# The expert stage's shift summed by VectorE instead of TensorE, in the projections of a diffusion trunk

## What is computed

```python
sh1, sc1, g1, sh2, sc2, g2 = adaln(cond, w_mod, b_mod)   # silu(cond) @ w_mod + b_mod, split in six
mix = mixer(modulate(rms_norm(x, g_attn), sh1, sc1))     # projections, heads A, B, C, output projection
x = x + g1 * mix
x = x + g2 * hier_moe(modulate(rms_norm(x, g_ffn), sh2, sc2))
```

## Time and profile before

| | us |
|---|---|
| median of 3 runs | 1699.66 |
| lowest, highest of the 3 | 1699.25, 7877.1 |
| the profiled execution | 1700.76 |
| its span, first to last instruction | 1698.9 |
| TensorE busy | 1592.4 (94%) |
| VectorE busy | 690.6 (41%) |
| ScalarE busy | 262.5 (15%) |
| GpSimd busy | 105.6 (6%) |

### The profile page before, as it was taken

One profiled execution on the slowest core, in us unless ns is written; L12 is line 12 of the kernel. 1 busy time (PEld: TensorE's weight loads), 2 busy tenths in 40 slices (PEclk: granted clock), 3 DMA queues, 4 the chain that ended last, 5 costly groups with the idle time before them and its releaser, 6 DMA issues.

```text
span 1698.9 us, 18207 instructions
## 1 busy us (share of the span) xinstructions
PE 1592.4 (94%) x6671; PEld 653.5 (38%) x6716; DVE 690.6 (41%) x1361; ACT 262.5 (15%) x705; POOL 105.6 (6%) x191
## 2 busy tenths in 40 slices
PE   4999999999999999999999998999999989999998
PEld 2445555544434444443332332333333233233332
DVE  2112232213245794443453344345344443534444
ACT  2003222112123010011101101111110110111010
POOL 1022100010020100000000000000000000000000
PEclk9999999999999999999999999999999999999999
DMA  9995642734199766589999999999999999999996
GB/s 367 385 341 220 230 192 65 265 111 181 68 359 406 266 264 254 187 340 426 427 429 427 429 426 427 427 426 428 428 424 428 427 425 424 428 426 426 419 427 246
DMA packets 92638, 581.94 MB, mean 343 GB/s; under 512 B 9113, under 2 KB 24313, under 8 KB 55385
## 3 DMA queue, kind: packets, MB, share of 16 engines
q1 hardware_dynamic: 84944, 554.20, 80.2%
q0 software_dynamic: 5920, 22.63, 3.6%
q10 hardware_dynamic: 1728, 4.51, 0.7%
HBM read 584.06 MB, written 7.05 MB: 348 GB/s over the span
## 4 chain that ended last, share of the span: by engine, by line
PE 67%; DMA 17%; DVE 4%; issue 1%; ACT 1%; SPq 0%; POOL 0%; ACTq 0%
PE bank L1284 23%; DMA ring<-in_w 17%; PE bank L1032 13%; PE bank L1011 7%; PE bank L1194 7%; PE bank L1317 3%; DVE r L1778 2%; PE bank L906 2%; PE bank L1119 2%; PE bank L1243 2%; PE bank L1180 1%; PE bank L1266 1%; PE bank L992 1%; PE bank L1094 1%; PE bank L1102 1%
## 5 line engine op out<-in xcount | busy, mean ns | idle before, releaser
L1284 PE MATMUL bank<-ring,r 128*64 128x512 f32 x1920 | 469.2, 618 | 45.1 <-DMA ring<-in_w 45.1
L1284 PEld LDWEIGHTS bank<-ring,r 128*64 128x64 f32 x1920 | 129.6, 139 | 302.8 <-issue 302.8
L1032 PE MATMUL bank<-ring,r 128*128 128x384 f32 (+1 forms) x672 | 240.7, 516 | 0.0
L1998 DVE TENSOR_TENSOR bank<-bank,r 128x512 f32<-128x512 f32 x180 | 125.9, 700 | 265.7 <-PE bank L1194 265.7
L1317 PE MATMUL bank<-ring,mod_row 128*64 128x512 f32 x896 | 195.8, 593 | 8.1 <-ACT mod_row L1531 7.9
L1011 PE MATMUL bank<-ring,r 128*128 128x512 f32 x384 | 170.0, 595 | 0.0
L1032 PEld LDWEIGHTS bank<-ring,r 128*128 128x128 f32 x672 | 126.1, 190 | 102.9 <-issue 43.2
L1194 PE MATMUL bank<-r 128*128 128x512 bf16 x495 | 137.6, 382 | 7.2 <-issue 7.2
L2000 DVE TENSOR_TENSOR r<-r,bank 128x512 f32<-128x512 f32 x180 | 123.6, 687 | 6.2
L1317 PEld LDWEIGHTS bank<-ring,mod_row 128*64 128x64 f32 x896 | 75.2, 137 | 119.0 <-issue 108.9
L1194 PEld LDWEIGHTS bank<-r 128*128 128x128 bf16 x540 | 38.0, 97 | 167.4 <-DVE r L2000 96.5
(11 more groups left out here) (279 smaller groups left out, 1249.9 us busy)
## 6 DMA issues: line engine op xcount, KB each, us to landing
ring<-in_w SPq DMA_DIRECT2D x180, 2048.0 KB, 18.1
ring<-in_w_mod SPq DMA_DIRECT2D x96, 1024.0 KB, 14.1
ring<-in_w SPq DMA_DIRECT2D x19, 1024.0 KB, 10.1
ring<-in_w_o SPq DMA_DIRECT2D x16, 1024.0 KB, 7.3
ring<-in_w_in SPq DMA_DIRECT2D x20, 768.0 KB, 13.3
ring<-in_w_in SPq DMA_DIRECT2D x8, 1024.0 KB, 6.0
r<-mod_d POOLq DMA_DIRECT2D x8, 1024.0 KB, 9.1
r<-in_w SPq DMA_DIRECT2D x5, 1024.0 KB, 8.3
```

The costliest lines, as they stand in the source:

```text
L1032: mm = pe.matmul(acc[acc_of(a)][:, 0:w], h_t[:, k, t * P:(t + 1) * P], wu[:, j, :], start=(k == 0), stop=(k == KD - 1))
L1284: mm = pe.matmul(ps[64 * c:64 * c + 64, :], xg_t[:, j, 64 * c:64 * c + 64], big_cut(slot_of(u), (8, 512))[:, j % 8, :], start=(j == 0), st ...
L1998: v.tensor_tensor(ps[:, :], ps[:, :], g2b[:, min(t, 1), cols], ALU.mult).then_inc(strip_scaled, 1)
```

## The change

SH2 leaves TensorE's modulation steps, and `LATER_GROUPS` becomes (G1, SH2, SC2). Sixteen steps ("sh2", k) stand in the list instead, each directly behind a projection job (its norm where that comes at once, and the turn due then): one behind every tile of cq1, aq0, bq0, akv and bq1, and one behind aq1 tile 2. VectorE does two multiply-adds 128x2048 in each, as for G2. The two partial sums live in two ring slots, which GpSimd sets to zero and starts with the bias rows, and which are kept out of the ring from cq1's first weights until ten units behind the fold; the ring has ten slots meanwhile (`ring_plan` instead of `ring_slot`). With two groups left in `later`, the three steps in cq1 tiles 1 and 2 and the two behind aq0 tile 1 are gone, and `mods(2)` before a group of heads is `mods(1)`. After the last A heads, a step "fold" has TensorE sum both over the partitions with eight products into `mod_ps`; VectorE copies the result and GpSimd stores it.

```diff
-LATER_GROUPS = (SH2, G1, SC2)
+LATER_GROUPS = (G1, SH2, SC2)
+SH2_AT = {"cq1": (1, 1, 1), "aq0": (1, 1, 1), "aq1": (0, 0, 1), "bq0": (1, 1, 1), "akv": (1, 1, 1), "bq1": (1, 1, 1),
+          "bkv": (0, 0, 0)}
...
-def ring_slot(m):
+def ring_plan(n, held_from, held_to):
+
+    def run(names):
+        at, prior, order, last, held = [], [], list(names), {}, []
+        for m in range(n):
+            if m == held_from:
+                held, order = order[:2], order[2:]
+            if m == held_to:
+                order = held + order
+            s = order.pop(0)
+            order.append(s)
+            at.append(s)
+            prior.append(last.get(s))
+            last[s] = m
+        return at, prior, order, held
...
-    later = [(g, k) for g in LATER_GROUPS for k in range(KD)]
+    later = [(g, k) for g in LATER_GROUPS if g != SH2 for k in range(KD)]
+    sh2 = iter(range(KD))
...
             n = len(jobs) - 1
+            for k in [next(sh2) for _ in range(SH2_AT[name][t])]:
+                units.append(("mod", SH2, k))
+                steps.append(("sh2", k))
             if name == "cq1":
...
-                else:
-                    mods(3)
                 job("proj", ("cq0", t))
                 kvc(t + 1, 0)
                 kvc(t + 1, 1)
             else:
-                mods(2 if attends and (name, t) != ("bkv", 2) else 0)
+                mods(1 if attends and (name, t) not in (("bkv", 2), ("aq0", 1)) else 0)
...
     assert not scored and not turned_p
+    steps.append(("fold", SH2))
+    held_to = len(units) + SLOTS - 2
     steps.append(("cache", "b"))
...
+    held_from = unit_no[("first", FIRST_GROUPS[1], 3, 3)] + 1
...
+        sh2_sum = [ring[:, s, :] for s in held]
...
+        def emptied(m):
+
+            if m >= held_to and prior[m] < held_from and slots[m] in held:
+                return row_out, 2 * 32
+            return frees[prior[m]]
...
-                if m >= SLOTS:
-                    sp.wait_ge(*frees[m - SLOTS])
+                if prior[m] is not None:
+                    sp.wait_ge(*emptied(m))
...
+            def fold_sh2():
+
+                pe.wait_ge(*frees[unit_no[("mod", SH2, KD - 1)]])
+                pe.wait_ge(mod_read, 1)
+                for c in range(2):
+                    for q in range(4):
+                        mm = pe.matmul(mod_ps[32 * q:32 * q + 2, :], K("sel")[:, c:c + 2], sh2_sum[c][:, q * 512:(q + 1) * 512],
+                                       start=(c == 0), stop=(c == 1))
+                mm.then_inc(mod_done, 1)
...
+            def sh2_step(k):
+
+                m = unit_no[("mod", SH2, k)]
+                if k == 0:
+                    v.wait_ge(sh2_rows_in, 2 * 16)
+                v.wait_ge(*full_of(m))
+                for c in range(2):
+                    if c and k:
+                        v.wait_ge(*frees[unit_no[("mod", SH2, k - 1)]])
+                    last = v.scalar_tensor_tensor(out=sh2_sum[c], in0=ring[:, slots[m], :], scalar=csil[:, k, c:c + 1],
+                                                  in1=sh2_sum[c], op0=ALU.mult, op1=ALU.add)
+                    if c == 0:
+                        after(last)
+                last.then_inc(*done_of(m))
...
+                elif s[0] == "fold":
+                    v.wait_ge(mod_done, 2)
+                    v.tensor_copy(sh2_sum[0][:, 0:512], mod_ps[:, :]).then_inc(mod_read, 1)
...
             load_row(LATER_GROUPS[0])
+            for slot in held:
+                g.wait_ge(*frees[max(m for m in range(held_from) if slots[m] == slot)])
+            g.memset(sh2_sum[0], 0.0)
+            after(g.memset(sh2_sum[1], 0.0))
+            for c in range(2):
+                g.dma_start(sh2_sum[c][0:1, :], b_rows[SH2:SH2 + 1]).then_inc(sh2_rows_in, 16)
...
+                elif s[0] == "fold":
+                    g.wait_ge(mod_read, 2)
+                    for c in range(2):
+                        g.dma_start(mod_d[SH2, c].rearrange("(q n) -> q n", q=4), sh2_sum[0][c:P:32, 0:512]).then_inc(row_out, 16)
```

More of the change, by code:

```diff
@@ L79 @@
 FOLD_AT = 6
-RING_FROM = 8
-def ring_slot(m):
-    return (m + RING_FROM) % SLOTS
+def ring_plan(n, held_from, held_to):
[12 more added lines that the diff above has]
+        return at, prior, order, held
+    end = run(range(SLOTS))[2]
+    name = [end.index(s) for s in range(SLOTS)]
+    at, prior, end, held = run(name)
+    assert end == list(range(SLOTS))
+    return at, prior, held
 def const_layout():
@@ L296, in plan @@
     assert g2_k == KD
-    return steps, jobs, atts, units
+    return steps, jobs, atts, units, held_to
 IN_NAMES = ["x_prompt", "x_sample", "cache_a_k", "cache_a_v", "cache_b_k", "cache_b_v", "cache_c_kv",
@@ L310, in build @@
 def build(nc, ins, outs):
-    steps, jobs, atts, units = plan()
+    steps, jobs, atts, units, held_to = plan()
     lay, n_const = const_layout()
@@ L315, in build @@
     n_static = len(units)
+    held_from = unit_no[("first", FIRST_GROUPS[1], 3, 3)] + 1
+    slots, prior, held = ring_plan(n_static + FIRST_UNITS - (EXTRA[1] - EXTRA[0]), held_from, held_to)
     n_jobs, n_atts = len(jobs), len(atts)
@@ L668, in build @@
                     else:
-                        slot_uses[ring_slot(u)] += 1
+                        slot_uses[slots[u]] += 1
         uses = [0] * SLOTS
@@ L672, in build @@
             if u not in frees:
-                uses[ring_slot(u)] += 1
-                frees[u] = (slot_free[ring_slot(u)], uses[ring_slot(u)])
+                uses[slots[u]] += 1
+                frees[u] = (slot_free[slots[u]], uses[slots[u]])
         assert uses == slot_uses
@@ L684, in build @@
                 done = [unit_no[("mod", G2, s[1])]]
+            elif s[0] == "sh2":
+                done = [unit_no[("mod", SH2, s[1])]]
             elif s[0] in ("proj", "kvc", "out"):
@@ L716, in build @@
             else:
-                slot_uses[ring_slot(m)] += 1
-                frees[m] = (slot_free[ring_slot(m)], slot_uses[ring_slot(m)])
+                slot_uses[slots[m]] += 1
+                frees[m] = (slot_free[slots[m]], slot_uses[slots[m]])
         def first_place(u):
             if u in first_no:
-                return ring[:, ring_slot(first_no[u]), :]
+                return ring[:, slots[first_no[u]], :]
             return extra[u - EXTRA[0]]
@@ L731, in small_free @@
         def small_free(u):
-            slots = (2 * slot_of(u), 2 * slot_of(u) + 1)
-            return [frees[max(m for m in frees if ring_slot(m) == slot)] for slot in slots]
+            pair = (2 * slot_of(u), 2 * slot_of(u) + 1)
+            return [frees[max(m for m in frees if slots[m] == slot)] for slot in pair]
         def moe_free(u, m):
@@ L1007, in out_part @@
                 arrived(m)
-                wu = cut(ring_slot(m), (4, 512))
+                wu = cut(slots[m], (4, 512))
                 for j in range(4):
@@ L1015, in out_part @@
                 elif t == TILES - 1:
-                    mm.then_inc(slot_free[ring_slot(m)], 1)
+                    mm.then_inc(slot_free[slots[m]], 1)
             a = 0
@@ L1777, in g2_step @@
                         v.wait_ge(*frees[unit_no[("mod", G2, k - 1)]])
-                    last = v.scalar_tensor_tensor(out=g2_sum[:, c, :], in0=ring[:, ring_slot(m), :], scalar=csil[:, k, c:c + 1],
+                    last = v.scalar_tensor_tensor(out=g2_sum[:, c, :], in0=ring[:, slots[m], :], scalar=csil[:, k, c:c + 1],
                                                   in1=g2_sum[:, c, :], op0=ALU.mult, op1=ALU.add)
+                    if c == 0:
[11 more added lines that the diff above has]
+                                                  in1=sh2_sum[c], op0=ALU.mult, op1=ALU.add)
                     if c == 0:
```

44 lines of the change are left out of this document (24 added, 20 removed).

## The result

The changed kernel takes 1717.47 us in the median of 4 runs (1716.74 to 1721.43), the kernel before 1700.57 beside it (one of its four executions took 7877.1 us; the median of the other three is 1699.66): ratio 1.0104, 95% interval 1.0088 to 1.012. That is 17 us or 1% slower, in the range of the prediction and 4.8 us above its point. The profiled execution took 1717.73 us around a span of 1715.9, 17.0 more than before.

A forecast was written before the change was run, and what follows sets the result against it. TensorE bounds the kernel up to the experts, the weight stream in them. Delays 3.6 + 0.9 + 4.1 + 4.1, less 0.5, 0.1 and 6.0, plus fold 1.8 and clock 5.1, give 13.0 us slower: 1712.7 us, range 1704 to 1719.

The forecast's parts named there:

- The three delays: In cq1's tiles 0, 1, 2, VectorE's blocks make norms late for TensorE's transposes: 3.6 plus 0.9, 4.1 and 4.1 us.
- GpSimd held, 0.9: In cq1 tile 0, kvc (0,0)'s rstd on GpSimd is held to the block's end, delaying the norm another 0.9 us.
- The clock, 5.1: Behind cq1's three new long TensorE waits the clock falls, 1.7 us each, 5.1 us in all.
- What is won back, 6.6: Steps removed from TensorE gain 0.5 us at first C heads, 0.1 before first A heads, 6.0 in seven other pairs.
- the other seven halves of pairs give 0.86 each: Where one of two consecutive SH2 steps leaves TensorE, seven places each save 0.86 us, 6.0 us together.
- some 5: Sign of being right: from the first C heads to the last A heads some 5 us are won back.
- The fold, 1.8: After the last A heads, TensorE's eight products summing the partial sums add 1.8 us, with no wait counted.
- The slots, 0: Ten ring slots from cq1's weights to the fold cost 0; bq0 tightest, but the DMA row is low there.
- GpSimd held in cq1's tiles 1 and 2 too: Rival: GpSimd is held there by one multiply-add each, 4.7 us more, 1717.4 us; chance 0.07.
- weights late: Rival: ten slots leave bq0 waiting 2.7 us, and blocks past the fold as much again, 1718 us; chance 0.08.
- the clock didn't hold: Refers to the rival that the clock holds around cq1's waits, leaving 7.9 us, 1707.6 us; chance 0.25.
- The relief that wins: Rival: no block reaches TensorE at cq1's transposes, so 14.1 less 1.8 us stays saved, 1687.4 us; chance 0.1.

The follow-up runs named there:

- the short fillers: Changed kernel plus idle TensorE products, fewer than the waits are long (3 or 6), ahead of five turns in cq1's stage: 1714.2 us, ratio 1.0081.
- the blocks ahead: Changed kernel with cq1's three blocks summed by VectorE ahead of the next projection's products instead of between a projection's results and their transposes: 1702.64 us, ratio 1.0003.
- the first block ahead: Changed kernel with only cq1's first block moved ahead of cq1 tile 1's products, those of tiles 1 and 2 staying: 1715.09 us, ratio 1.0088.
- the same with own turns: Changed kernel with cq1's three blocks moved ahead, and heads waiting only for ScalarE's copy of their own kind's last turn: 1700.86 us, ratio 0.9995.
- the waits filled too long: Changed kernel with 6, 10 and 10 idle TensorE products in its three long cq1 waits: 1725.78 us, ratio 1.014.

## Why the prediction held, point by point

**The three delays** (3.6 + 0.9, 4.1, 4.1). Bare, they are 3.94, 4.04 and 4.03 us. Tiles 1 and 2 are right to 0.1, though the removed steps, which I had at 0.7 us net of waiting, gave 0.49 and 0.51 when they alone were taken away. Moving the blocks shows the cause. Of the forecast's own signs, the projection that started at 173.40 starts 9.6 us later (8 or more), and the waits were 5.29, 4.41 and 3.63 us in the first profile (4 to 5), but 5.28, 2.70 and 2.72 in the second, where the slow clock filled part of them.

**GpSimd held, 0.9.** The mechanism is there (0.27 to 2.25 us, and 2.72 for the next), the price too high. I had the first operation held to the block's end and its 1.0 us of successors behind it. In the trace one operation is long beside each multiply-add, so they ran beside the block and the norm started at 153.81, 0.2 us behind the key's part that I had at 153.6. Beside the 3.6, 0.3 is left for this term in the bare 3.94. The rule of the Trainium skill, SBUF — State Buffer, "Who interferes with whom", that a VectorE instruction with two SBUF inputs and a GpSimd one that reads SBUF exclude each other for an instruction's length, agrees with the trace: both operations' lengths, 2.25 and 2.72 us, are near one multiply-add's 2.35.

**The clock, 5.1.** This term was mis-sized: 6.9 in one profile, 6.1 in the next. Three falls of 1.7 had been assumed; against the short fillers a stretch lost 0.0 to 3.0, and behind the third long wait the fall reaches into the next projection. I had priced the long waits alone; the clock also fell behind the wait of 2.15 us that was left in tiles 1 and 2, once in the first profile and twice in the second.

**What is won back, 6.6.** The step that failed is "the other seven halves of pairs give 0.86 each". In the changed kernel one gives 0.85 (bq1's tile 1), six 0.28 to 0.38, together 2.75 instead of 6.0. Their second step had covered ScalarE's copy of the turn, for which the first score waits by the plan. With that wait loosened all six are worth 0.85 or 0.86. The first C heads gave 0.23 instead of 0.5, bq1's tile 0 gave 0.34 instead of 0.1. All in all 3.3 (I had 6.6, and "some 5" among the signs).

**The fold, 1.8.** 1.68: from the fold's start to the output projection it took 41.12 us; the same piece before, from the cache turn at 492.85 us, which stands there without a fold, took 39.44. The fold's row took what G2's took the earlier trace rows:

```profile
508.41 1.90 PE L1014 MATMUL bank<-ring,cst 128*2 128x512 f32 x16
```

**The slots, 0.** Right for the changed kernel, where TensorE waits for no transfer there. But in the kernel before ten slots made it wait 0.78 us in bq0, so the argument "the DMA row is low there" was not a safe one.

**The sum.** A to D: 5.34 + 4.41 + 7.06 + 2.12 = 18.9; less 3.3; plus 1.7: 17.3. The first product of the output projection starts at 549.53 instead of 532.29, 17.24 later, and from there to the end the two profiles take 1166.4 and 1166.6 us: the shift is carried to the end one to one, as assumed. That they agree to 0.2 us is luck, since this last part took from 1164.4 to 1170.7 us in the twelve profiles, and 1169.1 in the changed kernel's second. Against the forecast's 13.0 that is 4.3 too much: 3.3 of relief that did not come and 1.8 of clock, less 0.7 in the three delays (12.0 instead of 12.7) and 0.1 in the fold.

The two large errors point the same way, so they didn't cancel: 1717.5 lies near the upper edge of the range and outside the forecast's own 1709 to 1716.

**The rivals.** By the time alone the rivals at 1717.4 (GpSimd held in cq1's tiles 1 and 2 too) and 1718 (weights late) fit better than the forecast; the traces rule them out. In tile 1 a GpSimd operation is indeed held, but VectorE goes on with cq0's norm as soon as the block is over, and the two stretches without the clock's part are 4.04 and 4.03 us longer, where I had 4.1 without it. These are GpSimd's row and VectorE's, block and norm:

```profile
175.76 2.60 POOL L2180 TENSOR_TENSOR small<-small,cst 128x2 f32<-128x2 f32 x1
...
175.46 4.74 DVE L1837 SCALAR_TENSOR_TENSOR ring<-ring,csil 128x2048 f32<-128x2048 f32 x2
180.12 1.01 DVE L1870 SCALAR_TENSOR_TENSOR r<-r,small,gains 128x64 f32<-128x64 f32 x4
```

TensorE waited for no weights, and the clock didn't hold. The relief that wins, priced at 14.1 - 1.8 = 12.3 us, is much smaller even where no block is in the way: with the blocks ahead the five stretches are 3.3 us shorter than before, and the output projection starts 2.5 sooner. In the whole time not even that shows (1.0003, 0.9993 to 1.0013); where it goes behind the projections stays open.

## What to carry to other kernels

Work moved to an engine that is busy 45% of the time is priced by its place in that engine's order: the same block cost 4 us between a norm and its transposes, and nothing ahead of the products. Work removed from the busiest engine is worth only what no other engine needs: ask for each removed piece which copy or norm it covered (here 0.5 of 2.7 us and 0.3 to 0.4 of 0.86 were left), and loosen or move that wait with it. Where the gain is under 0.3%, compare stretches of the profile; the whole time hides it, and a gain in a stretch may not reach the end.

## What the runs showed of the hardware

A wait costs twice. Behind the waits of 5.29, 4.41 and 3.63 us in the changed kernel's first profile, and of 5.28, 2.70 and 2.72 us in its second, TensorE's granted clock stood at 0.50 for a while, for 6 to 7 us beside 12 of lateness. Idle products in the waits took that away (6.9 us in the stretch), without making anything earlier.

A short wait may or may not bring a fall. Cq1's tiles 1 and 2 have a wait of 2.15 us each in six profiles (the changed kernel's two, the first block ahead, the blocks ahead, the same with own turns, the waits filled too long): behind six of these twelve the clock fell. The wait of 1.56 us at the first C heads stands in eight profiles, and in two of them, both with fillers in cq1, the clock fell behind it. So the clock isn't to be booked as a fixed price per wait. The Trainium skill, TensorE: Matmul & The Clock Gate, "HAM oscillation — how this bites in real kernels", says that idle gaps between bursts of products bring the slower level back, every time anew; the traces agree for the long waits, while the falls behind 1.56 and 2.15 us show that shorter ones are not safe.

With two slots fewer of twelve the kernel before took 2.9 us more (1.2 to 4.4), of which the trace gives 1.05 to a transfer waited for (0.78 us) in bq0; the rest is open.
